# Attention units alternate between two score areas by size, and ScalarE takes over the squares

## The reference, cut to what matters

```python
scale = DA_HEAD_DIM ** -0.5
s = jnp.einsum('bqhcd,bkhcd->bchqk', q_blk, k) * scale
mask = cid[None, :] <= c_blk[:, None]
p = jax.nn.softmax(jnp.where(mask, s, NEG_INF), axis=-1)
w = p[:, 0] - lam * p[:, 1]
return jnp.einsum('bhqk,bkhe->bqhe', w, v)
...
o = o * lax.rsqrt(jnp.mean(o * o, -1, keepdims=True) + LN_EPS) * subln_g.astype(F32)
return (o * (1.0 - lam_init)).reshape(bsz, L, DA_WIDTH)
```

## Time and profile before

| what | us |
|---|---|
| runs before, median (lowest to highest of 3) | 2460.54 (2460.26 to 2462.5) |
| the profiled execution's span | 2463.3 |
| TensorE busy | 2234.1 (91%) |
| VectorE busy | 776.3 (32%) |
| ScalarE busy | 475.8 (19%) |
| first instruction of the attention to the last scaled result | 350.9 to 555.6 |

### The profile page before, as it was taken

One profiled execution on the slowest core, in us unless ns is written; L12 is line 12 of the kernel. 1 busy time (PEld: TensorE's weight loads), 2 busy tenths in 40 slices (PEclk: granted clock), 3 DMA queues, 4 the chain that ended last, 5 costly groups with the idle time before them and its releaser, 6 DMA issues. The chain is left out here.

```text
span 2463.3 us, 33586 instructions
## 1 busy us (share of the span) xinstructions
PE 2234.1 (91%) x13475; PEld 1269.7 (52%) x13475; DVE 776.3 (32%) x1637; ACT 475.8 (19%) x884; POOL 308.1 (13%) x263
## 2 busy tenths in 40 slices
PE   5999978889968999999976999999986999999994
PEld 4687535565545455455533555555544555545541
DVE  5652026554352111111116344444233111111116
ACT  2222114341110000000003344442110000001001
POOL 5343000001101111101003000000100101111102
PEclk9999988789978999999988999999987999999997
DMA  4100010002229999989979211102118999998987
GB/s 152 36 4 32 17 71 1 1 1 57 72 104 390 419 419 420 419 335 406 412 298 310 93 39 38 38 19 54 52 51 350 413 419 420 420 389 353 417 369 293
DMA packets 148201, 529.82 MB, mean 215 GB/s; under 512 B 43875, under 2 KB 66947, under 8 KB 131665
## 3 DMA queue, kind: packets, MB, share of 16 engines
q1 hardware_dynamic: 119232, 490.78, 50.4%
q0 software_dynamic: 13312, 33.84, 3.6%
q10 hardware_dynamic: 15504, 3.08, 0.6%
HBM read 499.99 MB, written 39.98 MB: 219 GB/s over the span
## 5 line engine op out<-in xcount | busy, mean ns | idle before, releaser
L1787 PE MATMUL l_main_pgu<-l_w_ring,l_ex_xT 128*64 128x256 f32 (+1 forms) x4992 | 472.8, 384 | 12.7 <-DMA l_w_ring<-in_l_moe_w_gate 9.5
L1787 PEld LDWEIGHTS l_main_pgu<-l_w_ring,l_ex_xT 128*64 128x64 f32 (+1 forms) x4992 | 285.2, 128 | 189.6 <-issue 40.5
L1833 PE MATMUL l_main_py<-l_w_ring,l_ex_hT 128*64 128x512 f32 (+1 forms) x1248 | 231.9, 595 | 1.9 <-DVE l_ex_hT L1904 1.9
L1784 PE MATMUL l_main_pgu<-l_w_ring,l_ex_xT 128*128 128x512 f32 x384 | 170.1, 596 | 4.8 <-DMA l_w_ring<-in_l_moe_w_gate 4.8
L2245 PE MATMUL lru_pr<-h2T,lru_wz 128*128 128x352 f32 (+1 forms) x480 | 144.3, 461 | 11.6 <-ACTq L2300 11.6
L1900 DVE TENSOR_TENSOR l_ex_hid<-l_ex_sil,l_main_pgu 128x256 f32<-128x256 f32 (+1 forms) x76 | 35.2, 463 | 376.9 <-PE l_main_pgu L1787 279.7
L1904 DVE COPY l_ex_hT<-l_main_ph 128x256 f32<-128x256 f32 (+1 forms) x76 | 35.4, 466 | 366.4 <-PE l_main_ph L1808 366.4
L2263 PE MATMUL lru_pg<-h2T,lru_wz 128*128 128x512 f32 x320 | 148.7, 592 | 0.0
L1833 PEld LDWEIGHTS l_main_py<-l_w_ring,l_ex_hT 128*64 128x64 f32 (+1 forms) x1248 | 69.1, 127 | 132.1 <-issue 124.8
L2245 PEld LDWEIGHTS lru_pr<-h2T,lru_wz 128*128 128x128 f32 x480 | 92.6, 193 | 64.4 <-ACTq L2300 12.0
L1876 ACT ACTIVATE l_ex_sil<-l_main_pgu 128x256 f32<-128x256 f32 (+1 forms) x76 | 31.7, 417 | 468.9 <-PE l_main_pgu L1787 373.2
(11 more groups left out here) (450 smaller groups left out, 2785.2 us busy)
## 6 DMA issues: line engine op xcount, KB each, us to landing
l_w_ring<-in_l_moe_w_gate SPq DMA_DIRECT2D x64, 2048.0 KB, 24.4
l_w_ring<-in_l_moe_w_up SPq DMA_DIRECT2D x64, 2048.0 KB, 30.5
l_w_ring<-in_l_moe_w_down SPq DMA_DIRECT2D x64, 2048.0 KB, 32.5
l_y<-expert_rows SPq DMA_DIRECT2D x32, 512.0 KB, 8.3
h_rows<-H SPq DMA_DIRECT2D x24, 512.0 KB, 5.2
lru_wz<-in_l_w_in SPq DMA_DIRECT2D x20, 512.0 KB, 5.0
H<-h_rows SPq DMA_DIRECT2D x16, 512.0 KB, 10.1
w_in<-in_l_w_in SPq DMA_DIRECT2D x3, 2048.0 KB, 8.1
```

Source lines behind the costliest of these rows:

```text
L1784: last = pe.matmul(out[:], x[:, k, :], w[0][:, k, :], start=k == 0, stop=k == KD - 1)
L1787: last = pe.matmul(out[HALF * h + o:HALF * h + o + m, 0:256], x[:, k, it.at + o:it.at + o + m], w[n][:, k, 256 * h:256 * h + 256], start=k ...
L1833: last = pe.matmul(py[b][HALF * h + o:HALF * h + o + m, :], hT[:, c % 2, HALF * (c // 2) + o:HALF * (c // 2) + o + m], ws[n][:, c, 512 * h ...
```

## The change

**Order.** All heads' units are split in two lists: wide ones (tiles 4 to 8 in even heads, 8 to 5 in odd ones) and narrow ones (3 to 0 in even heads, 0 to 4 in odd ones), 18 each, and taken in turn: wide, narrow, wide, narrow. The pairs of two heads are, in keys, 528/400, 656/272, 784/144, 912/16, 1040/16, 1040/144, 912/272, 784/400, 656/528, and the same again for the other two heads. What each engine does within a step stays as it was.

**Areas.** There are two score areas, [2, 1024] for the wide units and [2, 512] for the narrow ones, six banks as before. scores(u) waits for both exps of unit u-2. The last 16 keys of a unit that does not fit (1040 keys in 1024, now also 528 in 512: six units rather than four) go to the end of the other area, in the scores of the unit before, and `copy_tail` brings them to `scores_tail_sb` one step early. ScalarE takes the exp of these 16 first and that of the area second.

**Squares.** `square` is gone from VectorE; ScalarE's `out` makes the scaled copy and then a Square with the same scale from the bank `weighed`, with its sum into `o_ss`. `o_copied` comes behind both.

**Start.** The first unit's minima and exps come before the wait for the small parameters.

```diff
+    wide = [(hd, qi) for hd in range(HEADS) for qi in ((4, 5, 6, 7, 8) if hd % 2 == 0 else (8, 7, 6, 5))]
+    narrow = [(hd, qi) for hd in range(HEADS) for qi in ((3, 2, 1, 0) if hd % 2 == 0 else (0, 1, 2, 3, 4))]
+    units = [unit for two in zip(wide, narrow) for unit in two]
...
-        S = [ctx.enter_context(nc.psum_tensor(f"scores{i}", [P, WIDE], F32)) for i in range(3)]
+        S = [ctx.enter_context(nc.psum_tensor(f"scores{i}", [P, 2, n], F32)) for i, n in enumerate((WIDE, NARROW))]
...
+        tail_place = lambda u, m: S[(u - 1) % 2][0:m, :, room[u - 1] - N_META:room[u - 1]]
...
-                if u:
-                    pe.wait_ge(exp_done, 2 * u - 1)
-                if n > WIDE and u > LAG + 1:
-                    pe.wait_ge(o_copied, u - LAG - 1)
...
+                if u >= 2:
+                    pe.wait_ge(exp_done, 2 * u - 2)
+                if u >= 2 and tailed[u - 1]:
+                    pe.wait_ge(tail_done, tails[u])
+                if u + 1 < U and tailed[u + 1]:
+                    tail_scores(u + 1)
...
-                act.mul(o_sb[0:m, qi, P * hd:P * hd + P], po[0:m, :], r[0:m, u % 4, 0:1]).then_inc(o_copied, 1)
+                if u == 0:
+                    act.wait_ge(cleared, 2)
+                act.mul(o_sb[0:m, qi, P * hd:P * hd + P], po[0:m, :], r[0:m, u % 4, 0:1])
+                act.activation(sq[0:m, u % 2, :], po[0:m, :], ACT.Square, scale=r[0:m, u % 4, 0:1], accum_out=ss[0:m, qi, hd:hd + 1]).then_inc(o_copied, 1)
...
+                if u == -1:
+                    act.wait_ge(lam_ready, 2)
+                    act.activation(lexp[:], ldot[:], ACT.Exp).then_inc(lexp_done, 1)
...
+            def copy_tail(u):
+                m = TILES[units[u][1]][1]
+                dve.wait_ge(tail_made, 2 * tails[u + 1])
+                dve.wait_ge(s_ready, 2 * u)
+                if tails[u]:
+                    dve.wait_ge(exp_done, 2 * last_tail(u) + 2)
+                dve.tensor_copy(tail_sb[0:m, :, :], tail_place(u, m)).then_inc(tail_done, 1)
+                dve.wait_ge(tail_done, tails[u + 1])
...
-            def square(u):
-                hd, qi = units[u]
-                m = TILES[qi][1]
-                dve.wait_ge(o_copied, u + 1)
-                if u >= 2:
-                    dve.wait_ge(squared, u - 1)
-                o = o_sb[0:m, qi, P * hd:P * hd + P]
-                dve.tensor_tensor_reduce(sq[0:m, u % 2, :], o, o, 1.0, 0.0, ALU.mult, ALU.add, ss[0:m, qi, hd:hd + 1]).then_inc(squared, 1)
```

More of the change, by code:

```diff
@@ L661, in attention @@
+    units = [unit for two in zip(wide, narrow) for unit in two]
     U = len(units)
+    room = [(WIDE, NARROW)[u % 2] for u in range(U)]
+    keys = [sum(TILES[qi]) for _, qi in units]
+    held = [min(n, r) for n, r in zip(keys, room)]
+    tailed = [n > r for n, r in zip(keys, room)]
+    assert U == HEADS * NT and not tailed[0]
+    assert all(keys[u] <= room[u] + N_META and keys[u - 1] <= room[u - 1] - N_META for u in range(U) if tailed[u])
     groups = [-(-(qi + 1) // PER) for _, qi in units]
@@ L691, in cuts @@
             q0, m = TILES[units[u][1]]
-            n = q0 + m
-            ends = list(range(0, n, 512)) + [n]
-            return q0, m, n, list(zip(ends, ends[1:]))
+            return q0, m, keys[u], held[u]
         @block.tensor
@@ L698, in _ @@
             pe.wait_ge(hide_made, 4)
+            rows = [slice(64 * c, 64 * c + 64) for c in range(2)]
             def scores(u):
                 hd, qi = units[u]
[L703 to L720 removed]
+                q0, m, n, h = cuts(u)
+                if u >= 2:
[4 more added lines that the diff above has]
+                    tail_scores(u + 1)
+                seen = n - 64 if qi else n
+                ends = list(range(0, h, 512)) + [h]
+                for a, b in reversed(list(zip(ends, ends[1:]))):
+                    lo = max(a, seen)
+                    for c in range(2):
+                        last = pe.matmul(S[u % 2][0:m, c, a:b], K.qT[rows[c], hd, q0:q0 + m], K.kT[rows[c], hd, a:b], start=True, stop=lo >= b)
                         if lo >= b and a == 0:
@@ L724, in scores, with tail_scores @@
                         for c in range(2):
-                            last = pe.matmul(place(c, lo, b), hide[rows[c], 0:m], ones[rows[c], 0:b - lo], start=False, stop=True)
+                            last = pe.matmul(S[u % 2][0:m, c, lo:b], hide[rows[c], 0:m], ones[rows[c], 0:b - lo], start=False, stop=True)
                             if a == 0:
                                 last.then_inc(s_ready, 1)
+            def tail_scores(u):
+                hd, qi = units[u]
+                q0, m, n, h = cuts(u)
+                place = tail_place(u, m)
+                for c in range(2):
+                    pe.matmul(place[:, c, :], K.qT[rows[c], hd, q0:q0 + m], K.kT[rows[c], hd, h:n], start=True, stop=False)
+                for c in range(2):
+                    pe.matmul(place[:, c, :], hide[rows[c], 0:m], ones[rows[c], 0:n - h], start=False, stop=True).then_inc(tail_made, 1)
             def turn(u, j):
```

81 lines of the change are left out of this document (39 added, 42 removed).

## The result

The changed kernel takes **2478.17 us** (median of 4 runs, 2474.25 to 2479.91) beside 2460.85 before (4 runs): ratio 1.0072, 95% interval 1.0058 to 1.0087. It is slower by 17 us. The profiled execution spans 2477.8, 14.5 more than that of before. Of the executions of the kernel before that were taken beside the experiments, one took 7060.98 us and is left out of the ratios.

A forecast was written before the change was run, and what follows sets the result against it. No engine was full: a chain through TensorE, VectorE and ScalarE was taken to bound the attention loop. Start 353.8, loop 195.6 and end 7.5 sum to 556.9 against 555.6 before, so 2462 us; range 2449.5 to 2475.

The forecast's parts named there:

- Start: Ahead of the loop: third step ends at 365.9, so the loop starts in effect at 353.8, 7.3 us sooner.
- The pairs at full clock: Attention loop: nine wide/narrow pairs of 6.9 to 12.2 us sum to 85.7, four heads 171.4 us at 2.4 GHz.
- the prediction's formula: Attention loop: at a share x of low clock it takes 171.4 / (1 - 0.325 x) us.
- longer at any clock: Attention pairs: a rival from the experiments, that pairs are simply longer whatever the clock; no size or chance given.
- x = 0.38: Attention loop: assumed share of time at 1.2 GHz, near the 0.41 before, giving a loop of 195.6 us.
- Some twelve: Wide steps with the first copy on VectorE: TensorE waits 2.2 to 3.6 us, some twelve times in 18 pairs.
- End: Behind the last step of the sum: the last unit, now 528 keys, takes 7.5 us to its scaled result.
- Squares: ScalarE's added Square per unit: 0.38 us on the chain in twelve of 18 pairs, 4.6 us within the sum.
- Rival 2: Wide steps, behind VectorE's copy and ScalarE's second exp and square: waits keep the clock down, slower, 2475 us; chance 0.29.
- Rival 1: Behind each wait in the loop: dense work restores the clock at once, x 0.2, faster, 2449.5 us; chance 0.22.
- Rival 3: Weighing in the loop: the result is never waited for, weighing starts on TensorE's side everywhere, 2450.5 us; chance 0.11.
- Rival 4: ScalarE in each unit: Square needs another table than Exp, two loads per unit, 92 us, 2554 us; chance 0.01.

The follow-up runs named there:

- s1: The changed kernel with the wait for the small parameters back ahead of the first minima and exps: 2475.1 us, ratio 1.0057 to before.
- e7: The changed kernel with ScalarE taking the narrow unit's result ahead of its second exp in wide steps: 2464.16 us, ratio 1.0015 to before.
- f4: The kernel before with VectorE's first-group copy between the minima and the result ahead of the second exp, except at 1040 keys: 2447.68 us, ratio 0.9963.
- e2: The kernel before with only the new order of units, wide and narrow alternating: 2487.98 us, ratio 1.0116 to before.
- f3: The kernel before with only VectorE's copy of a first group moved between the two minima: 2447.39 us, ratio 0.9938 to before.
- f2: The changed kernel with first-group copy between minima, narrow result before second exp, narrow scores inside wide steps, squares on VectorE: 2441.02 us, again 2440.02.

## Why the prediction was wrong, point by point

Forecast 556.9 for the last result, found 578.95: 22.1 us late (21.7 by the scaled row itself). By the terms of its sum:

- **Start.** 353.8 from a third step that ends at 365.9: it ended at 365.26. Right as a time; that it is worth 7.3 us was wrong, by s1: 2.8 at that step and nothing at the end.
- **The pairs at full clock.** Two pairs ran all but wholly at 2.4 GHz: 784 keys behind 912 from 438.26 to 446.97, 8.7 (8.5 forecast; the row at 446.97 is the first behind its weighing), and 656 behind 528 from 471.83 to 479.20, 7.4 (6.9).

```profile
438.26 0.73 PE L725 MATMUL scores<-kT,qT 64*128 64x272 f32 x4
...
446.97 0.40 PE L740 MATMUL scores<-kT,qT 64*128 64x16 f32 x4
...
471.83 0.52 PE L725 MATMUL scores<-kT,qT 64*128 64x144 f32 x4
...
477.70 1.57 PE L766 MATMUL weighed<-v_rows,w_cols 16*128 16x128 f32 x10
```

  No pair of 1040 keys ran so. The first two took 15.0 (395.36 to 410.40) and 14.6 (to 425.02), with the clock low in 0.55 and 0.51 of them; the prediction's formula makes 14.6 and 14.6 of its 12.0 and 12.2, an estimate. So nothing points at the 171.4 as the step that failed, and the rival "longer at any clock" is not borne out, though only two of the nine lengths were seen at full clock.
- **The share of low clock: the step that failed.** x = 0.38 was taken near before's 0.41, because six us of dense work lie behind each wait. From 353.8 to 565.9, the end of the last pair, the clock is 0.74, a share of 0.52. The formula then gives 171.4 / (1 - 0.325 x 0.52) = 206.3, +10.7. The reason given was the mistake: the dense work did not bring the clock back in time, it ran at the low level (eight tiles in 4.05 us from 406.42).
- **The price of low clock.** The pairs took 212.1, another 5.8. The formula spreads low time evenly over a pair (0.325 us for each low one); in truth TensorE was busy in 88% of it, which at half speed is up to 0.44 for each. 110 low us by the difference is up to 12.7, so the 5.8 lies within. The pair of 656 keys behind 784 (446.97 to 460.33), low in 0.63 of it, took 13.4 where the formula makes 11.8 of its 9.4, and the next, 528 behind 656, low in 0.76, took 11.5 against 10.6: the excess does lie in pairs that were mostly low. That the formula's even spread is the reason was argued, not run apart.
- **How many waits.** "Some twelve" long waits of 2.2 to 3.6 us were expected. Waits of 2 us or more for a copy came eight times, the longest 3.09, four of them for VectorE and four for ScalarE; the transposes waited 21 times in all, 11 for VectorE (17.3 us) and 10 for ScalarE (16.7). So the long waits were fewer and shorter than forecast, and the low time was larger all the same. For ScalarE's copy had shown 0.85; in wide steps that copy, too, stands behind the long exp.
- **End.** 7.5 expected, 13.05 found, all at 1.2 GHz: it was priced at a full clock. +5.6.
- **Squares.** 4.6 us within the sum; 2.8 and 4.1 by the runs, neither with intervals apart. Near in size as far as these tell, and the sign is shown on the old order alone. The wait for them came in 8 places, not twelve, at 1.1 us in the mean. The rule of the Trainium skill, "ScalarE: Activation LUTs", section "Rules for kernel authors", that multiplications belong on VectorE, the runs agree with on the old order: the squares on ScalarE cost 0.19% (0.06 to 0.33). In the changed kernel the medians point the same way, not clear of noise.
- **The rest of the kernel.** "What follows the loop is unchanged" was wrong by 8.8 us in the profiles (1907.6 to 1898.9), which hid part of the loss.

The sum: 10.7 + 5.8 + 5.6 = 22.1 (parts of one trace: that they add up proves none of them). Less the 8.8 behind the loop it is 13.3, and by the medians the forecast was 16.4 too low (2478.2 against 2461.8).

Rival 2 was the case, by its place and mechanism; its 2475 was 3 us short, since price and end were undersized and the faster part behind the loop did not make up for them, and so was the range's top. Rival 1's short falls did not come. Rival 3's gain exists (e7: 14 us) in the changed kernel; on the old order it was tried only together with the moved copy and outside the steps of 1040 keys (f4), and added nothing there. Rival 4 is out: one table load ahead of the exps, one behind the loop. Of the signs listed, these came: no scores wait for the exp of the unit before, no wait for squares on VectorE, the first exps stand at 355.15 ahead of the parameters.

**Open:** why the time behind the loop differs. From the start of the last scaled result to the end of the profile it is between 1898.4 and 1908.5 us, 1899.6 both after the longest loop but one (e2) and in the changed kernel, 1908.5 in f3 and 1908.0 in e7, and 1903.0 and 1900.3 in two profiles of the same kernel (f2). It follows neither the loop's end nor one edit; no run set it apart.

## What to carry to other kernels

When TensorE shares a loop with slower engines, price a wait by what it does to the clock as well as by its length: here 11 us of one wait less (7 of idle time) were worth 27. Do not take the share of low clock over from the old order; ask of each new wait what stands behind it, since dense work there runs at the low level. And before reordering units, look where in each engine's order the small operation stands that TensorE waits for: one copy moved ahead of a long minimum gained 13 us on the old order, where the reordered kernel lost 17 and, with its waits mended, was not shown to beat that copy.

## What the runs showed of the hardware

Waits filled with 35.6 us of useless matmuls made the kernel 19 us faster than leaving them empty, and raised the mean granted clock of the loop from 0.73 to 0.92. The wait of 3.09 us ahead of 403.00 was followed by a fall at 404.18, and the clock was back at 411.01, in time for the next wait; a wait of 2.05 us ahead of 429.95 was also followed by a fall, at 431.49. A Square of 128x128 from the bank costs ScalarE 0.36 + 0.20 us, next to VectorE's 0.28 + 0.08 from the scaled copy.
